# Four layer norms of a decoder trunk: normalising chunk by chunk beside the last output stage

## The reference

```python
x = layer_norm(DN_ALPHA * x + y, ln_g[layer, 0], ln_b[layer, 0])
x = layer_norm(DN_ALPHA * x + sq_relu_mlp(x, w_up, w_down), ln_g[layer, 1], ln_b[layer, 1])

def layer_norm(x, g, b):
    mu = mean(x, -1)
    var = mean(square(x - mu), -1)
    return (x - mu) * rsqrt(var + LN_EPS) * g + b
```

## Time and profile before

| | |
|---|---|
| median of 3 runs | 3373.28 us (3372.2 to 3375.8) |
| the profiled execution | 3373.14 us, of which its span is 3371.3 us |
| TensorE matmul busy | 3227.9 us, 96% of the span |
| VectorE busy | 1978.9 us, 59% |
| ScalarE busy | 1000.0 us, 30% |
| GpSimd busy | 869.2 us, 26% |
| mean granted TensorE clock | 0.967 of full speed |

### The profile page before, as it was taken

The page is one execution under the profiler, slowest core; times in us unless marked ns, Lnnn a source line. Parts: engine busy times, 40 slices in busy tenths (PEclk is TensorE's granted clock), DMA queues, the critical chain, the costliest instruction groups (busy, mean ns, idle before and its releaser), DMA issues.

```text
span 3371.3 us, 51878 instructions
## 1 busy us (share of the span) xinstructions
PE 3227.9 (96%) x20874; PEld 3091.5 (92%) x20874; DVE 1978.9 (59%) x2897; ACT 1000.0 (30%) x2433; POOL 869.2 (26%) x394
## 2 busy tenths in 40 slices
PE   7999999999996999999999899999987999999997
PEld 7899999999996999999998888888866999999996
DVE  6677777777777733443445767666667634333336
ACT  4544444444441311111110343443433211111112
POOL 2111111111111343333333222222201433343331
PEclk9999999999997999999999899999987999999997
DMA  3111111111110114311111322222210111111111
GB/s 115 54 45 54 59 55 56 47 61 56 43 62 15 38 45 150 132 63 44 45 50 38 97 76 82 76 76 82 80 47 13 51 44 47 48 45 51 44 51 51
DMA packets 86370, 201.11 MB, mean 60 GB/s; under 512 B 9416, under 2 KB 47176, under 8 KB 85616
## 3 DMA queue, kind: packets, MB, share of 16 engines
q1 hardware_dynamic: 35552, 139.54, 12.1%
q10 hardware_dynamic: 50592, 58.37, 5.6%
HBM read 166.86 MB, written 39.60 MB: 61 GB/s over the span
## 4 chain that ended last, share of the span: by engine, by line
issue 64%; PE 21%; POOLq 6%; POOL 6%; SPq 1%; DVE 1%; ACT 0%; DMA 0%; DVEq 0%; ACTq 0%
PE jb L364 21%; POOL wl L323 6%; POOLq L333 6%; SPq L302 1%; PE aux L546 0%; DVEq L1313 0%; ACT acc L1063 0%; DMA wraw<-in_wstream 0%; DVE acc L1314 0%; DVE acc L1560 0%; DMA acc<-in_xT 0%; POOLq L347 0%; POOLq L330 0%; DVE lnq L1564 0%; DVE xl L1312 0%
## 5 line engine op out<-in xcount | busy, mean ns | idle before, releaser
L364 PE MATMUL jb<-xh,wh 128*128 128x344 f32 x2616 | 843.1, 322 | 7.2 <-POOL wl L323 3.7
L364 PE MATMUL jb<-xl,wh 128*128 128x344 f32 x2616 | 837.2, 320 | 0.0
L364 PE MATMUL jb<-xh,wl 128*128 128x344 f32 x2616 | 837.0, 320 | 0.0
L323 POOL TENSOR_TENSOR wl<-wraw,wh 128x1024 fp32r<-128x1024 f32 x225 | 550.1, 2445 | 845.7 <-ACT wh L882 822.4
L331 POOL TENSOR_TENSOR wh<-wraw,one 128x1024 fp32r<-128x1024 f32 x164 | 318.8, 1944 | 1591.3 <-PE jb L364 887.1
L1344 DVE TENSOR_TENSOR acc<-jb,acc 128x344 f32<-128x344 f32 x504 | 254.4, 515 | 449.1 <-PE jb L364 445.5
L364 PEld LDWEIGHTS jb<-xh,wh 128*128 128x128 f32 x2616 | 493.0, 188 | 8.9 <-POOL wl L323 4.5
L364 PEld LDWEIGHTS jb<-xh,wl 128*128 128x128 f32 x2616 | 492.9, 188 | 0.0
L364 PEld LDWEIGHTS jb<-xl,wh 128*128 128x128 f32 x2616 | 492.8, 188 | 0.2
L364 PE MATMUL jb<-hh,wh 128*128 128x344 f32 x1536 | 492.2, 320 | 0.0
L364 PE MATMUL jb<-hl,wh 128*128 128x344 f32 x1536 | 490.9, 320 | 0.0
(11 more groups left out here) (271 smaller groups left out, 5049.3 us busy)
## 6 DMA issues: line engine op xcount, KB each, us to landing
wraw<-in_wstream SPq DMA_DIRECT2D x225, 512.0 KB, 3.2
pre<-in_state ACTq DMA_DIRECT2D x16, 512.0 KB, 4.3
out_ssm_s<-pre ACTq DMA_DIRECT2D x16, 512.0 KB, 3.5
kgat<-in_cache_k SPq DMA_DIRECT2D x16, 512.0 KB, 5.3
vgat<-in_cache_v SPq DMA_DIRECT2D x16, 512.0 KB, 6.5
past<-kgat ACTq DMA_DIRECT2D x8, 1024.0 KB, 5.8
past<-vgat ACTq DMA_DIRECT2D x8, 1024.0 KB, 5.7
acc<-in_xT SPq DMA_DIRECT2D x8, 516.0 KB, 6.7
```

Source lines behind the costliest of these rows:

```text
L323: nc.gpsimd.tensor_tensor(wl[slot][:], wraw[:, slot], wh[slot][:].bitcast(F32), ALU.subtract).then_inc(w_split, 1)
L364: last = mm(jb[:, c, 0:CW], w[slot][:, j * kt + k], x[:, k, cols], start=(k == 0 and p == 0), stop=(k == kt - 1 and p == 2))
```

## The change

Layer norms of a token chunk are interleaved with the last output stage before them and with the first chunks of the stage behind.

- **The last output stage goes by token chunk.** `by_chunk` computes all 8 jobs of chunk 0, then of chunk 1, then of chunk 2. So up to four units of weights stay in use for the whole stage; `home` gives them places besides the two slots (in `we`, and in the free part of `hh[0]`). The last head's output loop is turned in the same way.
- **Between its chunks stands the norm.** In the passes over chunks 1 and 2, `norm_beside` puts the mean of the chunk before behind the first job, its variance behind the fifth and its spread behind the seventh. Those of chunk 2 stand in `jobs_after_norm`, behind its first, fourth and fifth chunk. After norm 3 there is nothing more to stand beside.
- **`jobs_after_norm` takes three jobs** instead of two, 9 chunks in the order AFTER_NORM. After norm 1 the third is the first head's values.
- **Means.** In norms 0 and 2 DVE no longer sums the tiles; TensorE sums them from `acc` by 8 matmuls per chunk, fp32, 344 columns. In norms 1 and 3 the sums stay on DVE.
- **Scale, shift, low.** `scale` multiplies 4 tiles per instruction by the deviation alone; ACT applies gamma and beta, once into `xh` and once into `acc` (two ACTIVATE per tile instead of one); `low` takes 4 tiles per instruction. Alpha is applied by the first addition to `acc` in the next sub-layer, and the 8 instructions of L1605 are gone.
- **GpSimd's loop** over units is written out.

Three places of the order, before and after. `jb<-yh,wh` is a pass of the mixer's output, `aux` the PSUM banks of the norm, `x8` a row that stands for eight.

TensorE at norm 0, before: the whole of mean, variance and spread stands between the last output chunk and the first of the MLP (L579).

The core of the diff:

```diff
-UP_ORDER_AFTER_NORM = [(j, c) for c in range(NCH) for j in range(2)] + UP_ORDER[6:]
+AFTER_NORM = [(0, 0), (1, 0), (2, 0), (0, 1), (1, 1), (2, 1), (1, 2), (0, 2), (2, 2)]
+UP_ORDER_AFTER_NORM = AFTER_NORM + UP_ORDER[9:]
...
+        def home(u):
+
+            for first in LAST_DOWN:
+                if first < u < first + 4:
+                    return (extra, slots[0], spare(0))[u - first - 1]
+            for l, first in enumerate(AFTER):
+                if u == first + 2:
+                    return (extra, spare(1), extra)[l]
+            return slots[u % 2]
...
+            def split(u):
+                pool.wait_ge(raw_in[u % 2], 16 * (u // 2) + 16)
+                begun = u
+                for first in LAST_DOWN:
+                    if first < u < first + 4:
+                        begun = (first, first + 1, first + 1)[u - first - 1]
+                for l, first in enumerate(AFTER):
+                    if first <= u < first + 3:
+                        begun = ((first, first + 1, first), (first - 2, first, first))[l % 2][u - first]
+                if u > 1:
...
+            def mean(l, c):
+                pe.wait_ge(s["ln_sum"], 3 * l + c + 1)
+                cols = slice(c * CW, (c + 1) * CW)
+                if l % 2:
+                    mm(ln_bank(c)[:, 0:CW], ones[:, 0:P], ln0[:, cols], start=True, stop=True).then_inc(s["ln_mu"], 1)
+                else:
+                    for k in range(KD):
+                        last = mm(ln_bank(c)[:, 0:CW], ones[:, 0:P], acc[:, k, cols], start=(k == 0), stop=(k == KD - 1))
+                    last.then_inc(s["ln_mu"], 1)
...
+            def norm_beside(l, c, k):
+
+                if c and k == 0:
+                    mean(l, c - 1)
+                if c and k == 4:
+                    variance(l, c - 1)
+                if c and k == 6:
+                    spread(l, c - 1)
...
+            def by_chunk(l, at, kt, rh, rlo):
+
+                per = 8 // kt
+                weights = []
+                credits, _ = at.job(KD)
...
+                        x = c * KD + k
+                        if c == 0 and k % per == 0:
+                            _, nth = at.unit()
+                            pe.wait_ge(w_split, nth)
+                            weights.append(home(nth - 1))
+                        h, lo = weights[k // per]
+                        pe.wait_ge(bank_free[x % 3], credits + x // 3)
                         cols = slice(c * CW, (c + 1) * CW)
...
+                        for i in range(kt):
+                            for w, r, p in ((h, rh, 0), (h, rlo, 1), (lo, rh, 2)):
+                                last = mm(jb[:, x % 3, 0:CW], w[:, (k % per) * kt + i], r[:, i, cols],
+                                          start=(i == 0 and p == 0), stop=(i == kt - 1 and p == 2))
+                                if i == 0 and p == 0 and (x == 0 or c == 2 and k and k % per == 0):
                                     last.then_inc(unit_begun, 1)
                         last.then_inc(chunk_full, 1)
+                        norm_beside(l, c, k)
...
+                for x, (j, c) in enumerate(AFTER_NORM):
+                    if c == 0:
...
+                        if k % 4 == 0:
+                            pe.wait_ge(s["ln_lo"], 6 * l + 2 * c + 1 + k // 4)
+                        for w, r, p in ((h, xh, 0), (h, xl, 1), (lo, xh, 2)):
+                            last = mm(jb[:, x % 3, 0:CW], w[:, k], r[:, k, cols],
+                                      start=(k == 0 and p == 0), stop=(k == KD - 1 and p == 2))
+
+                            if k == 0 and p == 0 and x in (0, 7, 8):
+                                last.then_inc(unit_begun, 1)
+                    last.then_inc(chunk_full, 1)
+                    if x == 0:
+                        mean(l, 2)
+                    if x == 3:
+                        variance(l, 2)
+                    if x == 4:
+                        spread(l, 2)
...
-
-            layer_norm(0)
+                pe.wait_ge(s["h_ready"], (hb + FFB) * 12)
+                by_chunk(2 * layer + 1, at, 4, hh[1], hl[1])
+
+            by_chunk(0, after_scan, 2, yh, yl)
             mlp(0)
-            layer_norm(1)
 
...
+                        norm_beside(2, c, j)
...
             mlp(1)
-            layer_norm(3)
+            mean(3, 2)
+            variance(3, 2)
+            spread(3, 2)
...
+                def shift(c, g):
+
+                    act.wait_ge(s["ln_norm"], 6 * l + 2 * c + g + 1)
+                    cols = slice(c * CW, (c + 1) * CW)
+                    for k in range(4 * g, 4 * g + 4):
+                        g_, b_ = lnp[:, l, 0, k:k + 1], lnp[:, l, 1, k:k + 1]
+                        if l < 3:
+                            af(xh[:, k, cols], acc[:, k, cols], ACT.Identity, scale=g_, bias=b_)
+                        last = af(acc[:, k, cols], acc[:, k, cols], ACT.Identity, scale=g_, bias=b_)
+                    last.then_inc(s["ln_hi"], 1)
...
+                shift(1, 0)
+                evict(0)
+                shift(1, 1)
+                evict(1)
+                squares(2, 0)
+                squares(2, 1)
+                evict(2)
+                evict(3)
                 root(2)
+                evict(4)
+                shift(2, 0)
+                shift(2, 1)
+                evict(5)
...
 
-            at = Place(J_ATT, 0)
-            _, done = at.job(2)
-            for x, (j, c) in enumerate(UP_ORDER_AFTER_NORM[0:6]):
-                act.wait_ge(chunk_full, done + x + 1)
-                af((rawq, rawk)[j][:, c * CW:(c + 1) * CW], jb[:, x % 3, 0:CW], ACT.Copy,
-                   scale=(SCALE, 1.0)[j]).then_inc(bank_free[x % 3], 1)
+            def first_head(x):
+                j, c = AFTER_NORM[x]
+                act.wait_ge(chunk_full, 3 * J_ATT + x + 1)
+                af((rawq, rawk, rawv)[j][:, c * CW:(c + 1) * CW], jb[:, x % 3, 0:CW], ACT.Copy,
+                   scale=(SCALE, 1.0, 1.0)[j]).then_inc(bank_free[x % 3], 1)
+
+            layer_norm(1, first_head)
+            for x in range(6, 9):
+                first_head(x)
             queries_in(0)
             keys_in(0)
             act.wait_ge(s["gathered"], 16 * 2 * NB * PAGES)
             past_keys(0)
             act.wait_ge(s["lam_sum"], 1)
             af(lam[:, 0:2], lam[:, 0:2], ACT.Exp).then_inc(s["lam_exp"], 1)
...
+                if first:
+                    last = stt(acc[:, k, cols], acc[:, k, cols], ALPHA, jb[:, c, 0:CW], ALU.mult, ALU.add)
+                else:
+                    last = tt(acc[:, k, cols], jb[:, c, 0:CW], acc[:, k, cols], ALU.add)
...
+                def low(c, g):
+                    dve.wait_ge(s["ln_hi"], 6 * l + 2 * c + g + 1)
+                    v = at_chunk(c, g)
+                    tt(xl[v], acc[v], f(xh[v]), ALU.subtract).then_inc(s["ln_lo"], 1)
...
+                adds(0, 1, 2, 3, 4, 5, 6, 7)
+                adds(8)
                 drain()
-                centre(0)
-                centre(1)
+                centre(0, 0)
+                adds(9)
+                centre(0, 1)
+                adds(10, 11)
                 add_squares(0)
-                centre(2)
+                adds(12, 13)
                 invert_root(0)
+                adds(14, 15)
+
+                adds(16)
+                drain()
+                centre(1, 0)
+                adds(17)
+                centre(1, 1)
+                scale(0, 0)
+                adds(18)
+                scale(0, 1)
+                adds(19)
                 add_squares(1)
+                adds(20)
+                if l < 3:
+                    low(0, 0)
+                adds(21)
+                if l < 3:
+                    low(0, 1)
+                invert_root(1)
+                adds(22, 23)
                 drain()
-                scale(0)
-                invert_root(1)
+                if l == 3:
+                    centre(2, 0)
+                    centre(2, 1)
+                    scale(1, 0)
+                    scale(1, 1)
+                    add_squares(2)
+                    invert_root(2)
+                    scale(2, 0)
+                    scale(2, 1)
+                    return
+                scale(1, 0)
+                scale(1, 1)
+                centre(2, 0)
+                centre(2, 1)
+                low(1, 0)
+                up(0)
+                low(1, 1)
+                up(1)
                 add_squares(2)
-                low(0)
+                up(2)
+                up(3)
                 invert_root(2)
-                scale(1)
-                low(1)
-                scale(2)
-                low(2)
-                if l < 3:
-                    drain()
-
-                    for k in range(KD):
-                        ts(acc[:, k], acc[:, k], lnp[:, l, 1, k:k + 1], ALPHA, ALU.add, ALU.mult)
-                    drain()
+                up(4)
+                scale(2, 0)
+                scale(2, 1)
+                low(2, 0)
+                low(2, 1)
```

(6 more changed lines are left out.)

355 lines of the change are left out of this document (185 added, 170 removed).

## The result

The change makes the kernel slower: 3420.2 us median of 4 runs (3414.8 to 3421.0) against 3373.5 us before, a ratio of 1.0134, 95% interval 1.0117 to 1.0152. The forecast was 3405 us with a range of 3355 to 3425; the sign and the range held, the size was short by 15 us.

A forecast was written before the change was run, and what follows sets the result against it. TensorE, busy 96% of the span, was taken as the bound. Added work, remaining waits and half clock gave +9.0, +13.0, +10.1 and -0.5 us for norms 0 to 3: +31.6 on 3373.1, so 3405 us, range 3355 to 3425.

The forecast's parts named there:

- waits: TensorE idle at the norms' matmuls until DVE or ACT delivers: 71.1 us over four norms, in several short gaps.
- half clock: Short and wide matmuls behind TensorE's waits run at half clock: 42.5 us in all; upper bound 10 us more.
- the table's work: TensorE's work at full speed in the four norm windows: 92.1, 91.3, 80.8 and 57.4 us.
- lead-in: Ahead of the first head's scores: swaps, Exp table load and rotation, 16.7 us, no longer covered by the values; +12.7.
- tail: From the last chunk's spread to the kernel's end: 11.2 us in place of 13.4, -2.2.
- The means: In norms 0 and 2, 8 matmuls per mean in place of one, 4.6 us for 0.57, six times: +24.2 us.
- Rival A: Norm truly hidden: 38.5 us of waits beside the output stage and 23 of half clock vanish; 3345 us; chance 0.20.
- Rival B: Waits at the norms as walked, but the clock does not fall in them; 3376 us; chance 0.12.
- C: First head's lead-in stays covered because the last values are evicted during the swaps; 3392 us; chance 0.03.
- D: POOL's splits collide with DVE in the output stage, 1.7 us per hit, eight on the path; 3420 us; chance 0.07.

The follow-up runs named there:

- e5_one_tile_mean: The change, but in norms 0 and 2 the mean is one matmul from the first feature tile of acc alone; 3396.7 us, ratio 1.0068.
- e1_dve_sums: The change, but in norms 0 and 2 the means come from DVE's column sums and one matmul again; 3421.2 us, ratio 1.0138.
- e3_keep_clock: The change, but TensorE runs unused 256-column fp32 filler matmuls while it waits in the norms; 3400.0 us, ratio 1.0075.
- e9_wide_variance: The change, but a chunk's variance is 4 fp32 matmuls of 344 columns instead of 12 of one column, without spread; 3391.9 us, ratio 1.0044.
- e10_wide_fp32r: The change with earlier Exp and swaps, chunk 1's fold-before-scaling order, and variance by 8 fp32r matmuls straight from the squares, no fold or spread; 3353.4 us, ratio 0.9937.

## Why the prediction was right in sign and 15 us short

By the forecast's own table, measured in the profiled execution (waits are the idle times in brackets; half clock is the stretch less waits less the table's work):

| | waits: forecast, measured | half clock: forecast, measured | difference to before: forecast, measured |
|---|---|---|---|
| norm 0 | 17.3, 16.3 | 11.6, 15.7 | +9.0, +12.1 |
| norm 1 and lead-in | 16.7, 16.2 | 8.6, 14.1 | +13.0, +18.1 |
| norm 2 | 22.3, 20.2 | 14.0, 19.3 | +10.1, +13.3 |
| norm 3 and tail | 14.8, 13.9 | 8.3, 11.7 | -0.5, +3.2 |
| sum | 71.1, 66.6 | 42.5, 60.8 | +31.6, +46.7 |

- **The waits** held within 2.1 us in every norm, each at the place named. They came from walking the queues with durations of rows, drains and order included.
- **The half clock** is the step that was mis-sized: 42.5 forecast, 60.8 measured, more than the whole error of 15. The measured column is what is left over, so it holds other slow passes too. Counted matmul by matmul in the stretches granted 0.50, against the time of the same form at full clock, the loss is 14.7, 12.9, 17.6 and 10.5 us, 55.6 in all: still 13 over the forecast, and over its upper bound of 52.5. The forecast counted a lost variance and "some 1.3 to 2" us of wide passes behind each wait. After the wait ahead of chunk (1,2) 3.7 us were lost, and behind variances with a wait of only 0.8 us (norms 1 and 3) 1.6 to 1.9 us. The earlier trace rows show the clock at 0.50 through 24 us of short matmuls that are busy for 19, and the forecast drew from them that it does not recover during such work; that it also falls behind it, after next to no wait, none of the forecast's rows showed.
- **The lead-in** of 16.7 us stood exposed as forecast (16.7 measured), by its row. The tail came to 12.4 for 11.2: ScalarE's last activations.
- **The means**, +24.2, "all on TensorE and hence on the path. This is certain": e5_one_tile_mean confirms the price (22 us). But the sentence behind it, that DVE's sums matter only for how late DVE is, hid that this lateness is worth just as much here: e1_dve_sums. So the means do not explain the slowdown by themselves; in this order either way of summing costs some 22 us.
- **Rival A** (the norm truly hidden) asked for 32 of the 61 us of waits and clock beside the stage to go. Of its 38.5 us of waits 36.4 are there. Its premise that DVE has room was true on average (55% busy) and false at the places that count, where in-order scaling stands ahead of the fold. **Rival B** (the clock holds) fell by the windows. **C** was excluded by the row at 1944.48. **D** (collisions) has the measured time, 3420, but that is chance. It priced each hit on "an addition or sum", and only the sums of the earlier trace rows had shown one: the 16 additions `acc<-jb,acc` that ran beside a split in the norms 0, 1 and 3 took 0.52 us like the others. The waits, where hits would show, came out 4.5 us under the forecast in sum. At one place they did count: ahead of the 4.5 us wait at norm 1's second spread (forecast 3.3) a sum and a `low` beside splits took 1.92 and 3.72 us instead of 0.52 and 1.59:

```profile
1867.34 1.92 DVE L1476 TENSOR_TENSOR ln<-ln,acc 128x344 f32<-128x344 f32 x1
1869.18 3.72 DVE L1699 TENSOR_TENSOR xl<-acc,xh 128x1376 fp32r<-128x1376 f32 x1
```

- The Trainium skill's 81 ns per weight load and matmul pair at N = 128 ("TensorE: Matmul & The Clock Gate", "Back-to-back issue gap") was weighed against 114 ns and left. At a granted clock of 1.00 the 24 matmuls of a variance took 2.73 us (the row at 1124.32), 114 ns each, so the trace's figure was the right one.

What stays open: 5 to 6 us from one execution to the next of the same kernel. They may sit in where the clock falls; only one execution of each kernel has a trace, so that is not shown.

## What to carry to other kernels

Work put beside a busy engine is hidden only if no in-order queue makes that engine wait for it: count the waits at each meeting point, and then add the clock behind them (here 67 us of waits and 56 of half clock). Before overlapping a serial stage, shorten its chain. Here a variance by wide matmuls in place of one-column ones made the old, unoverlapped order 1.0% faster (3341 us), and the overlapped order with the same variance was no faster than that; it also had longer means and a longer lead-in to pay for. A mean over an engine's busy share says nothing of whether it is free at the moment when it is waited for.

## What the runs showed of the hardware

- Behind 24 one-column matmuls that kept TensorE busy (2.8 us at a granted 1.00, filler ahead of them), the next 2.7 us had a granted clock of 0.68 (e3_keep_clock); behind 4 fp32 matmuls of 344 columns it was 1.00, even after a wait of 5.3 us (e9_wide_variance). With a wait of 0.83 us ahead, 3.4 us at 0.50 followed the one-column form and none the wide one.
- DVE's reciprocal of 128 x 344 in PSUM took 2.31 us, nearly six times as long per element as its multiplication by a broadcast (1.58 us for 128 x 1376).
- Eight fp32r matmuls from squares written as fp32r by ScalarE took 1.3 to 1.4 us from their first start to the next matmul's at full clock (e10_wide_fp32r), against 2.2 for four tiles in fp32 (e9_wide_variance) and 1.58 for the fold on VectorE.
- Beside a GpSimd split VectorE's sum `ln<-ln,acc`, all in SBUF, took 2.1 us instead of 0.52 (median of 10 in the kernel before); the addition `acc<-jb,acc`, one operand in PSUM, took 0.52 in each of 199 such cases there.
